# A hybrid encoder layer on one core: the normalised input moved from 128 to 0 modulo 256 bytes in SBUF

## The reference: one layer, 512 tokens, width 1024, in float32

```python
x = x + 0.5 * swiglu(rms_norm(x, ffn1_norm[l]), ffn1_gate[l], ffn1_up[l], ffn1_down[l])
x = x + hybrid_mixer(rms_norm(x, mix_norm[l]), w_in[l], ...)
x = x + 0.5 * swiglu(rms_norm(x, ffn2_norm[l]), ffn2_gate[l], ffn2_up[l], ffn2_down[l])
return rms_norm(x, final_norm)
```

## The kernel before, in words

| tensor | modulo 256 | |
|---|---|---|
| xg_hi, xg_lo | 128 | tiles of 2,048 bytes, halves of 1,024 |
| w_hi, w_lo (both slots), first_hi, first_lo | 128 | rows of 512 bytes as stationary operand; as moving operand rows of 1,536 or 1,600 |
| h_lo, h_hi_s, h_hi_w, mixed_hi, mixed_lo | 128 | |
| s_hi, s_lo | 64 | behind a pad of 48 floats |
| sum_hi, sum_lo | 128 | behind a pad of 16 floats |
| dmat, glog_hi, glog_lo | 128 | |

## Time and profile before

### The profile page before, as it was taken

One profiled execution on the slowest core, in us unless ns is written; L12 is line 12 of the kernel. 1 busy time (PEld: TensorE's weight loads), 2 busy tenths in 40 slices (PEclk: granted clock), 3 DMA queues, 4 the chain that ended last, 5 costly groups with the idle time before them and its releaser, 6 DMA issues. The chain is left out here.

```text
span 955.0 us, 16547 instructions
## 1 busy us (share of the span) xinstructions
PE 943.2 (99%) x6290; PEld 843.6 (88%) x6290; DVE 677.2 (71%) x956; ACT 435.0 (46%) x686; POOL 358.0 (37%) x241
## 2 busy tenths in 40 slices
PE   9999999999999999999999999999999999999997
PEld 8889999999888889777899788889999999988887
DVE  6699999997643375677578964379999999833444
ACT  7564455555522223654534333544555545632331
POOL 0777776763010135110100014387767677000001
PEclk9999999999999999999999999999999999999999
DMA  6332324232232325222212122233232332222232
GB/s 210 120 102 90 130 88 132 88 121 71 99 100 100 102 76 175 75 74 78 76 52 68 45 89 91 86 132 111 89 129 91 115 104 91 86 100 77 100 100 89
DMA packets 31104, 94.27 MB, mean 99 GB/s; under 512 B 4464, under 2 KB 7712, under 8 KB 31056
## 3 DMA queue, kind: packets, MB, share of 16 engines
q1 hardware_dynamic: 29120, 90.28, 28.7%
q0 software_dynamic: 1648, 3.07, 1.2%
q10 hardware_dynamic: 288, 0.26, 0.1%
HBM read 90.38 MB, written 2.42 MB: 97 GB/s over the span
## 5 line engine op out<-in xcount | busy, mean ns | idle before, releaser
L1481 DVE TENSOR_TENSOR w_lo<-raw,w_hi 128x1024 fp32r<-128x1024 f32 (+2 forms) x128 | 193.8, 1514 | 147.1 <-ACT w_hi L1103 147.0
L1103 ACT ACTIVATE w_hi<-raw 128x1024 fp32r<-128x1024 f32 (+2 forms) x128 | 131.4, 1026 | 194.4 <-PE ps L570 194.3
L568 PE MATMUL ps<-xg_hi,w_hi 128*128 128x256 f32 (+1 forms) x528 | 178.2, 338 | 0.8 <-DVE w_lo L1481 0.6
L570 PE MATMUL ps<-xg_hi,w_lo 128*128 128x256 f32 (+1 forms) x528 | 175.0, 331 | 0.0
L569 PE MATMUL ps<-xg_lo,w_hi 128*128 128x256 f32 (+1 forms) x528 | 174.8, 331 | 0.0
L568 PE MATMUL ps<-s_hi,sum_hi 128*128 128x256 f32 x576 | 160.2, 278 | 2.5 <-ACT snap L1198 2.3
L569 PE MATMUL ps<-s_lo,sum_hi 128*128 128x256 f32 x576 | 159.4, 277 | 0.0
L570 PE MATMUL ps<-s_hi,sum_lo 128*128 128x256 f32 x576 | 159.2, 276 | 0.0
L569 PE MATMUL ps<-h_lo,w_hi 128*128 128x512 f32 x330 | 128.4, 389 | 0.0
L568 PEld LDWEIGHTS ps<-xg_hi,w_hi 128*128 128x128 f32 x528 | 99.9, 189 | 19.1 <-issue 8.2
L568 PEld LDWEIGHTS ps<-s_hi,sum_hi 128*128 128x128 f32 x576 | 108.4, 188 | 3.6 <-issue 3.4
(11 more groups left out here) (255 smaller groups left out, 1888.9 us busy)
## 6 DMA issues: line engine op xcount, KB each, us to landing
raw<-up_w SPq DMA_DIRECT2D x50, 512.0 KB, 4.0
raw<-down_w SPq DMA_DIRECT2D x38, 512.0 KB, 3.2
raw_u<-up_w SPq DMA_DIRECT2D x36, 512.0 KB, 3.2
raw<-t_w SPq DMA_DIRECT2D x15, 512.0 KB, 3.3
raw<-out_w SPq DMA_DIRECT2D x8, 512.0 KB, 3.3
raw<-nat_w SPq DMA_DIRECT2D x4, 576.0 KB, 3.8
x<-xT SPq DMA_DIRECT2D x8, 256.0 KB, 4.8
out<-x SPq DMA_DIRECT2D x8, 256.0 KB, 2.2
```

The source lines that it names most:

```text
L568: pe.matmul(out_ap, a[0], b[0], start=first, stop=False, skip_group_check=resumed)
L570: return pe.matmul(out_ap, a[1], b[0], start=False, stop=last, skip_group_check=resumed)
L1103: act.activation(dst, raw[:, slot(s), 0:w], ACT.Copy).then_inc(hi_ready, 1)
L1481: dve.tensor_tensor(lo, raw[:, slot(s), 0:w], hi, ALU.subtract).then_inc(lo_ready, 1)
```

## The change

Two pads are added around `xg_hi` and `xg_lo`, 32 floats (128 bytes) in front and 96 floats (384 bytes) behind. So both start at 0 modulo 256 bytes (256 modulo 512) where they started at 128, and everything behind them moves by 512 bytes and keeps its place modulo 512. No instruction is added, removed or reordered on any engine.

```diff
@@ -185,8 +185,10 @@
             return ctx.enter_context(nc.semaphore(name))
 
 
+        sb("below_xg", [P, 32])
         xg_hi = sb("xg_hi", [P, KT, S], F32R)
         xg_lo = sb("xg_lo", [P, KT, S], F32R)
+        sb("above_xg", [P, 96])
         w_hi = sb("w_hi", [P, 2, SLOTW], F32R)
         w_lo = sb("w_lo", [P, 2, SLOTW], F32R)
```

## The result

The changed kernel is slower: 959.83 us, median of 10 runs (957.01 to 960.37), against 956.40 before (956.10 to 957.01, 10 runs taken beside them). The ratio is 1.0025, with a 95% interval of 1.0016 to 1.0034. Not one run came near the 947.0 forecast.

A forecast was written before the change was run, and what follows sets the result against it. TensorE was taken as the bound, busy 943.2 of 955.0 us. Savings of 0.80 + 3.52 + 3.84 + 0.32 + 0.96 = 9.44 us off 956.84, less 0.42, gave 947.0 us; range 942 to 958.

The forecast's parts named there:

- This is offset / 4: Cycles lost per matmul equal the moving operand's offset from the 256-byte line over 4; at 0 nothing, saving 13.3 ns each.
- rival (c): Distance between moving and stationary operand counts, not place; if the new distance costs 64 cycles, 984 us; chance 0.17.
- It doesn't grow with the columns: The cycles lost per matmul are the same at 256 and 512 columns: 32 for the input at 128.
- my point at 64: `s`, starting at 64, has 256-column matmuls every 113.3 ns, 16 cycles lost: one of the points on the line.
- Start: The 60 input matmuls up to the mean squares, from 10.09 to 23.84 us: 0.80 us saved.
- Fast units: 18 in each FFN: unit falls from 9.76 to 9.69 us, 1.76 us saved per FFN, 3.52 together.
- the cap that I had named: In the fast units, DVE's own chain repeats every 9.69 us without waiting for TensorE, so units get no shorter.
- Late next: `snap`: In the fast units, `snap` and the gb part, behind ScalarE's split, are late next; TensorE's slack is 0.49 us.
- Mixer: Twelve transposed tiles, 374 to 474 us: 288 matmuls of 512 columns, 13.3 ns less each, 3.84 us saved.
- Second FFN's plain pairs: Three slabs of 24 matmuls on the path in the second FFN: 0.96 us saved.
- Natural sections: The input is the stationary operand there; the moving side stays at 128, so the change costs nothing either way.
- (a): Offset 0 is only as good as 64: 113.3 ns at 256 columns, 220 at 512; 950.2 us, chance 0.13.

The follow-up runs named there:

- The table: TensorE alone, layer left out: 16 pairings of moving and stationary places, 48 matmuls each at 512 and 256 columns; 226.6 to 233.3 ns at 512, 113.3 to 120.0 at 256.
- lower group: The changed kernel's faster runs: four of the ten, from 957.01 to 957.45 us; its first profiled execution (957.01 us) is one of them.
- the kernel at -64: Kernel before, with pads of 48 and 80 floats around the input, so that it starts at 64 modulo 256: 961.01 us, ratio 1.0046.
- the units at +64: Kernel before, with `sum` at 64, `s` at 0 and, in the fast units alone, weights 192 bytes further up in their slot: 954.47 us, ratio 0.9980.
- upper group: The changed kernel's slower runs: six of the ten, from 959.78 to 960.37 us; one was profiled when the kernel was run again, at 959.35 us.
- the two kernels with its distances: Kernel before with one 128-byte pad in front of everything: 956.81 us; kernel before with 256-byte pads in front of and behind the input: 956.35 us.

## Why the prediction was wrong, point by point

- **The step that failed** is the one in bold: "This is offset / 4". I drew it through three or four rows, and in all of them the stationary operand lies at 128, so they were rows of distance -64, 0 and a mix of 0 and +64. I wrote that under rival (c) ("no row separates place from distance") and still put 0.52 on place. Two further assumptions fell with it. "It doesn't grow with the columns": at the new distance, 232.4 ns are 46 cycles above 512 columns, 118.7 ns are 29 above 256. And that a distance has one price: `s` at 113.3 ns, my point at 64, is one of two patterns of its distance.
- The Trainium skill, "TensorE: Matmul & The Clock Gate", section "Step-by-step: what each phase is for", says that loading the next weights takes no read bandwidth from the running matmul. I let it count against (c). The table disagrees as far as time goes: with all else equal, the spacing of a matmul goes from 226.7 to 233.3 ns by where the operand lies that is loaded beside it. Whether it is bandwidth that they share, no run here shows.
- **Rival (c)** had the mechanism, at 0.17, and the wrong price: 64 cycles against 46 at 512 columns, and 29 instead of 64 at 256, where it is a gain of 3.
- Start, predicted -0.80: +0.07 at the first steady unit. From the row at 17.71 us to the product at 24.65 the matmuls take 6.94 us, in the changed kernel 7.11 (17.57 to 24.68); at 54.42 and 54.47 the two are nearly level.
- Fast units, predicted -1.76 each: -0.53 in each steady loop (and -0.33 at the second FFN's start) in the lower group. The term was mis-sized by the price: 36 matmuls at 118.6 ns, not 106.7, leave TensorE's own sum at 9.72 us, so the cap that I had named, DVE's chain of 9.69, wasn't reached in the changed kernel. The cap itself is real: in the eight units of the kernel at -64 in which both streams run at 113.3, TensorE stops at m7, and the unit is the chain's 9.67. With the units at +64 TensorE's sum and the chain are both 9.69, and can't be told apart. "Late next: `snap`" was right as well, in a way that I didn't foresee: a snapshot that came close stands ahead of each change of the pattern that was traced inside a loop.
- Mixer, predicted -3.84: +0.70, 2.4 ns each for 288, not the 5.7 of the table. In the kernel before, the runs of 12 between attention's hooks don't settle at 226.7 either (231, 235, 229, 232 ns from 399.11 us on), so there was less to lose. Second FFN's plain pairs, predicted -0.96: +0.63. Natural sections, "costs nothing either way": 173.3 to 175.8 ns at 384 columns, since for them the distance changes too.
- What no part of the prediction had is the largest part of the result: `s`, which the change doesn't touch, falls into a slower pattern for a loop: 2.6 us in the one that was traced, and by the groups of times in six of ten executions. Of the difference of 3.4 us between the medians that is the larger part; the upper group's other 0.4 to 1.0 were not traced.
- The way to tell stands in the prediction and worked: "113.3 and 220 (a), 133 and 240 (c)"; none of the four came. The unit was TensorE's own sum, 9.72.

## What to carry to other kernels

- Before a slope is drawn through rows, write down everything in which these rows are alike. If one operand lies in the same place in all of them, place and distance can't be told apart, and a short kernel of matmuls against a table of addresses settles it before the change is made.
- A stream of weight loads and matmuls is tuned as a pair: choose the distance of moving and stationary operand by the column count (0 for 512, +64 for 256 here), and let different stages have different ones, as slots with spare room allow.
- Look at all the times of a kernel, not only the median. Two tight groups with nothing between are two behaviours, and a profile shows one of them.
- Before a stream is made faster, see how little time lies between another engine's result and the matmul that needs it: here a result only 0.22 us ahead of it was followed by a loop that took 2.6 us more.

## What the runs showed of the hardware

- The start-to-start spacing of float32r matmuls, each with its own weight load, depends on the distance of the two operands modulo 256 bytes: 226.7 / 228.9 / 232.4 / 233.3 ns at 512 columns and 120.0 / 117.8 or 113.3 / 118.7 / 117.8 or 113.3 ns at 256, for 0, +64, 128, -64. Their places, and 256 against 0 modulo 512, make no difference (956.81 and 956.35 us against 956.7 and 956.6).
- A stream has more than one steady pattern. It keeps one for a whole loop of units, passes it on through runs of other operands, and can leave it at a single matmul that comes late (120 ns at 102.78 us, not healed; 144 ns at 112.18 us in another kernel, healed within five).
- The late matmuls of the traced loops stand where TensorE needs ScalarE's snapshot: all 15 units with 0.144 to 0.218 us between the snapshot's end and the matmul have one, and two of the 208 with more. Why three of the 15 changed the pattern for good and 12 healed stays open, and so does what a matmul and the weight load beside it share.
- Distance alone doesn't decide which pattern a loop keeps: by their times, units with equal distances fell into the slower pattern in 1 of 11 runs in one kernel and in 8 of 12 in another. In the kernel before and in the two kernels with its distances (11 runs each) no upper group showed.
